# One hybrid decoder layer: two weight rings of six slots, the low part written over the raw weights, in place of three rings of four

## The reference, cut to what matters

```python
h = rms_norm(x, norm_mix)
proj | gates = h @ w_in                       # 2048 x 3608 and 2048 x 6144
y_a, y_b, y_c = swa_attention(..), stick_breaking(..), nsa_attention(..)
merged = sum_i sigmoid(g_i) * (y_i @ w_branch_i)
x = x + merged @ w_out
h = rms_norm(x, norm_ffn)
x = x + (silu(h @ w_gate) * (h @ w_up)) @ w_down   # inner width 5632
out = rms_norm(x, norm_final)
```

## Time and profile before

| what | value |
|---|---|
| median of three runs | 1362.46 us |
| profiled execution, its own time | 1363.83 us |
| its span, first to last instruction | 1362.1 us |
| mean granted clock of TensorE | 0.999 |
| TensorE busy | 1350.7 us |
| VectorE busy | 950.6 us |
| ScalarE busy | 712.1 us |
| DMA | 261.08 MB, mean 192 GB/s |

### The profile page before, as it was taken

How to read it: one execution, slowest core, us unless ns; L and a number is a source line. 1 busy time by engine, 2 the same in 40 slices (tenths; PEclk the granted TensorE clock), 3 DMA queues, 4 the chain that set the end, 5 groups by cost and what they waited for, 6 DMA issues and landing times.

```text
span 1362.1 us, 26444 instructions
## 1 busy us (share of the span) xinstructions
PE 1350.7 (99%) x11247; PEld 1315.9 (97%) x11247; DVE 950.6 (70%) x1241; ACT 712.1 (52%) x927; POOL 44.8 (3%) x70
## 2 busy tenths in 40 slices
PE   8999999999999999999999999999999999999997
PEld 7888999999999999999999999999999999999997
DVE  6554456667654756767899899985546899988554
ACT  6333356656545664455655655544344555555444
POOL 3000010000000110000000000000000000000111
PEclk9999999999999999999999999999999999999999
DMA  7776555544565667555566666656556666666653
GB/s 244 248 229 223 181 170 156 155 140 141 156 188 167 194 204 225 182 187 171 185 194 197 220 195 190 198 197 208 199 189 189 196 214 191 194 192 230 211 194 124
DMA packets 135264, 261.08 MB, mean 192 GB/s; under 512 B 8448, under 2 KB 25408, under 8 KB 134768
## 3 DMA queue, kind: packets, MB, share of 16 engines
q1 hardware_dynamic: 132912, 251.13, 57.8%
q0 software_dynamic: 1792, 7.57, 1.6%
q10 hardware_dynamic: 448, 0.76, 0.2%
HBM read 257.33 MB, written 2.10 MB: 190 GB/s over the span
## 4 chain that ended last, share of the span: by engine, by line
PE 98%; DMA 1%; DVE 0%; ACT 0%; issue 0%; ACTq 0%; DVEq 0%
PE bank L649 26%; PE bank L651 25%; PE bank L650 25%; PE bank L888 5%; PE bank L891 5%; PE bank L890 5%; PE bank L637 3%; PE bank L787 1%; PE bank L698 1%; DMA raw_ring<-in_w_in 0%; DMA sigmoid_gates<-in_norm_mix 0%; PE bank L747 0%; PE bank L1011 0%; PE bank L699 0%; PE bank L835 0%; PE bank L813 0%
## 5 line engine op out<-in xcount | busy, mean ns | idle before, releaser
L1327 DVE TENSOR_TENSOR weight_lo_ring<-raw_ring,weight_hi_ring 128x1024 fp32r<-128x1024 f32 (+2 forms) x479 | 582.3, 1221 | 317.9 <-ACT weight_hi_ring L1071 260.4
L1071 ACT ACTIVATE weight_hi_ring<-raw_ring 128x1024 fp32r<-128x1024 f32 (+2 forms) x431 | 450.6, 1050 | 459.3 <-PE bank L651 299.5
L649 PE MATMUL bank<-weight_hi_ring,hT_hi 128*128 128x256 f32 (+2 forms) x1276 | 380.9, 298 | 0.0
L651 PE MATMUL bank<-weight_hi_ring,hT_lo 128*128 128x256 f32 (+2 forms) x1276 | 375.5, 294 | 0.0
L650 PE MATMUL bank<-weight_lo_ring,hT_hi 128*128 128x256 f32 (+2 forms) x1276 | 375.5, 294 | 0.0
L649 PEld LDWEIGHTS bank<-weight_hi_ring,hT_hi 128*128 128x128 f32 x1276 | 239.8, 188 | 10.0 <-issue 3.4
L650 PEld LDWEIGHTS bank<-weight_lo_ring,hT_hi 128*128 128x128 f32 x1276 | 239.9, 188 | 6.1
L651 PEld LDWEIGHTS bank<-weight_hi_ring,hT_lo 128*128 128x128 f32 x1276 | 239.6, 188 | 6.3
L649 PE MATMUL bank<-weight_hi_ring,h2T_hi 128*128 128x256 f32 x704 | 195.5, 278 | 0.0
L650 PE MATMUL bank<-weight_lo_ring,h2T_hi 128*128 128x256 f32 x704 | 194.6, 276 | 0.0
L651 PE MATMUL bank<-weight_hi_ring,h2T_lo 128*128 128x256 f32 x704 | 194.6, 276 | 0.0
(11 more groups left out here) (253 smaller groups left out, 1933.5 us busy)
## 6 DMA issues: line engine op xcount, KB each, us to landing
raw_ring<-in_w_in SPq DMA_DIRECT2D x96, 512.0 KB, 3.5
raw_ring<-in_w_gate SPq DMA_DIRECT2D x88, 512.0 KB, 4.3
raw_ring<-in_w_up SPq DMA_DIRECT2D x88, 512.0 KB, 4.2
raw_ring<-in_w_down SPq DMA_DIRECT2D x88, 512.0 KB, 4.0
raw_ring<-in_w_in SPq DMA_DIRECT2D x55, 480.0 KB, 4.2
raw_ring<-in_w_out SPq DMA_DIRECT2D x32, 512.0 KB, 4.0
raw_ring<-in_w_br_c SPq DMA_DIRECT2D x16, 256.0 KB, 3.8
raw_ring<-in_w_br_a SPq DMA_DIRECT2D x16, 256.0 KB, 6.5
```

The lines of the kernel that those rows point to most:

```text
L649: pe.matmul(dst, x_hi, w_hi, start=opening, stop=False, skip_group_check=True)
L651: m = pe.matmul(dst, x_lo, w_hi, start=False, stop=last and k == UK - 1, skip_group_check=True)
L1071: act.activation(whi[:, s, :, 0:width(u)], raw[:, s, :, 0:width(u)], ACT.Copy)\
L1327: dve.tensor_tensor(lo, w, hi.bitcast(F32), ALU.subtract).then_inc(lo_ready, 1)
```

## The change

`RING` becomes 6. `raw` and `whi` have six slots each, and `wlo` is placed at the address of `raw`, so the low part of a unit is written over its raw weights. The space is the same, 12 slots. A slot of `raw` is now free when TensorE has used the unit: the transfer of unit u waits for `unit_used >= u - 5`, the end of unit u-6. The high part of unit u waits for the end of unit u-6 as well, and for its transfer. The number of units kept for the last part stays four (`KEPT`). The three-round loops of the input projection are gone on all four engines; units 8 to 55 go through the same written-out code as the others, with its waits (TensorE waits at each chunk for its banks to be emptied). VectorE's two waits for constants come ahead of unit 8 in place of unit 56.

```diff
--- before.py
+++ after.py
@@ -51,7 +51,8 @@
 
 
 UK = 2
-RING = 4
+RING = 6
+KEPT = 4
 UPC = KD // UK
 N_QKV = -(-N_PROJ // WQ)
 U_MIX = N_QKV * UPC
@@ -250,9 +251,10 @@
             assert top[0] <= nc.sbuf_top, name
             return t
 
+        raw_at = top[0]
         raw = place("raw_ring", [RING, UK, W])
         whi = place("weight_hi_ring", [RING, UK, W], F32R)
-        wlo = place("weight_lo_ring", [RING, UK, W], F32R)
+        wlo = at("weight_lo_ring", [RING, UK, W], raw_at, F32R)
         ident = place("identity", [P])
         gainT = place("gains_T", [4, KD])
         sumsq = place("sumsq", [TT, NC_D])
@@ -468,7 +470,7 @@
                 sp.dma_start(raw[:, slot, :, :], src).then_inc(raw_ready[slot], 16)
 
             def free(count):
-                sp.wait_ge(lo_ready, count)
+                sp.wait_ge(unit_used, count)
 
             def straight(u):
                 q, j = CHUNK_OF[u]
@@ -504,22 +506,11 @@
                 cols = slice(X_PIECES[n][0], X_PIECES[n][1])
                 sp.dma_start(X[:, :, cols], x_b[:, :, cols]).then_inc(x_ready[n], 16)
 
-            for n in range(RING):
+            for n in range(len(X_PIECES)):
                 xload(n)
-                if n > 0:
+                if 0 < n < len(X_PIECES) - 1:
                     straight(n)
-            xload(RING)
-            for u in range(RING, UPC):
-                straight(u)
-            with sp.Fori(0, (N_QKV - 2) // 2) as i:
-                for c in range(2):
-                    for j in range(UPC):
-                        u0 = UPC + c * UPC + j
-                        sp.wait_ge(lo_ready, i * (2 * UPC) + (u0 - RING + 1))
-                        sp.dma_start(raw[:, u0 % RING, :, 0:WQ],
-                                     win_b[:, UK * j:UK * j + UK, bass.ds(i * (2 * WQ) + (1 + c) * WQ, WQ)])\
-                          .then_inc(raw_ready[u0 % RING], 16)
-            for u in range(U_MIX - UPC, U_FFN):
+            for u in range(len(X_PIECES) - 1, U_FFN):
                 straight(u)
             for u in range(U_FFN, U_END):
                 what, i, j = FFN[u - U_FFN]
@@ -961,7 +952,7 @@
                         pe.wait_ge(added, done)
                     if c == 0:
                         pe.wait_ge(aT_lo, 2 * (HALVES[h][0] + j // 2 + 1))
-                    if i == LAST_DOWN and j >= n - RING:
+                    if i == LAST_DOWN and j >= n - KEPT:
                         return
                     pe.wait_ge(lo_ready, u + 1)
                     products(u % RING, (actT_hi, actT_lo), c % 2, j == 0, j == n - 1, UK * j,
@@ -973,7 +964,7 @@
 
                 def finishing(t, halves):
 
-                    for j in range(n - RING, n):
+                    for j in range(n - KEPT, n):
                         u = AT["down", LAST_DOWN, j]
                         if t == 0:
                             pe.wait_ge(lo_ready, u + 1)
@@ -1035,18 +1026,7 @@
                     for a in range(1, 4):
                         m = transpose(bank[2][:, KD * a:KD * (a + 1)], rows[0:KD, a, :], KD)
                     m.then_inc(gains_full, 1)
-            with pe.Fori(0, (N_QKV - 2) // 2) as i:
-                for c in range(2):
-                    q0 = 1 + c
-                    if c == 0:
-                        pe.wait_ge(squares, 2 * NC_D)
-
-                    for j in range(UPC):
-                        u0 = UPC * q0 + j
-                        pe.wait_ge(lo_ready, i * (2 * UPC) + (u0 + 1))
-                        products(u0 % RING, (hT_hi, hT_lo), q0 % 2, j == 0, j == UPC - 1,
-                                 UK * j, WQ).then_inc(unit_used, 1)
-            for u in range(U_MIX - UPC, U_FFN):
+            for u in range(UPC, U_FFN):
                 straight(u)
                 follow(u)
             for u in range(U_FFN, U_END):
@@ -1075,13 +1055,6 @@
                     if n >= 2:
                         act.wait_ge(unit_used, SEVENS[n - 2] + 1)
                     act.activation(ext_hi[:, n % 2, :, :], t_sum[:, :, :], ACT.Copy).then_inc(ext_hi_ready, 1)
-
-            def split_in_loop(u0, rounds, units, cols=W):
-
-                s = u0 % RING
-                act.wait_ge(raw_ready[s], rounds * 16 + landed(u0))
-                act.wait_ge(unit_used, units + (u0 - RING + 1))
-                act.activation(whi[:, s, :, 0:cols], raw[:, s, :, 0:cols], ACT.Copy).then_inc(hi_ready, 1)
 
             def hi_of_transposed(n, b, dst, gain):
 
@@ -1276,10 +1249,7 @@
                 if m == 5:
                     gains(2, slice(1, 4))
             root(1)
-            with act.Fori(0, (N_QKV - 2) // 2) as i:
-                for j in range(2 * UPC):
-                    split_in_loop(UPC + j, i * (2 * UPC // RING), i * (2 * UPC), WQ)
-            for u in range(U_MIX - UPC, U_END + LAG):
+            for u in range(UPC, U_END + LAG):
                 if u < U_END:
                     split(u)
                 follow(u - LAG)
@@ -1710,18 +1680,10 @@
                     split(m)
             norm(1, TT * NC_D)
             dve.wait_ge(rstd_ready, 1)
-            with dve.Fori(0, (N_QKV - 2) // 2) as i:
-                for c in range(2):
-                    for j in range(UPC):
-                        u0 = UPC + c * UPC + j
-                        split_unit(u0 % RING, i * (2 * UPC) + (u0 + 1), WQ)
-                        if j == LAG - 1:
-                            dve.wait_ge(unit_used, i * (2 * UPC) + UPC * (1 + c))
-                            empty_projection(c, bass.ds(i * (2 * WQ) + c * WQ, WQ))
             dve.wait_ge(consts_ready, 1)
             dve.wait_ge(sinks_ready, 16)
 
-            for u in range(U_MIX - UPC, U_END + LAG):
+            for u in range(UPC, U_END + LAG):
                 if u < U_END:
                     split(u)
                 if u == U_MIX + LAG:
```

## The result

| | before | after |
|---|---|---|
| median of 18 runs each, us | 1362.41 (1361.87 to 1364.67) | 1365.18 (1363.40 to 1368.65) |
| profiled execution, its own time / span, us | 1363.83 / 1362.1 | 1366.62 / 1364.9 |

The ratio is 1.0019, 95% interval 1.0012 to 1.0025: 2.6 us slower, the interval lying on both sides of the 0.2% that the prediction took as no change. The forecast was 1363.9 with a range of 1361.0 to 1367.5.

A forecast was written before the change was run, and what follows sets the result against it. TensorE, busy 1350.7 of 1362.1 us, was taken as the bound, with one 0.3 us wait behind its first 7 us. Terms of 1.0 + 0.4 = 1.4 us on a median of 1362.46 gave 1363.9, range 1361.0 to 1367.5.

The forecast's parts named there:

- Pace of products: All weight units: reading low parts from the buffer that transfers fill costs 0, bounds 1.2 us gained to 1.2 lost.
- low part in place: VectorE writing the low part over the raw weights takes as long as into another tile: price 0.
- Loop written out: Input projection, units 8 to 55: the jumps cost nothing, so price 0, bounds 0 to 0.3 us.
- What moves: Steady units: requests go out 3.0 us later, yet low parts are ready 7.7 us before use, against 5.8.
- Place 1: End of the input projection: later request for unit 66 delays the transposes at L736, +1.0 us, bounds -0.3 to +1.4.
- Place 2: Second load of x, at 502.94 us: unit 171's weights queue behind it and may land late, cost 0.4 us (0 to 1.1).
- Place 3: Nine gate and up rounds with VectorE busiest: slack 1.5 us, priced 0, or 4.5 us if transfers take 5.4.
- Rival A: Gate and up rounds: above about 5.0 us latency each of nine loses the excess, 1368.4 us with 5.4; chance 0.14.
- The sum: Whole kernel: 1.0 + 0.4 = 1.4 us slower, median 1363.9 us; chance of the forecast 0.60.
- own bounds: Whole kernel: the gains of the terms give 1361.0 us, their losses 1366.5 us.
- The slow stretch at 682 us: 682 to 707 us: 213 products at 0.117 us each, some 1.2 us over the usual pace, unexplained, following late low parts.

The follow-up runs named there:

- e3: Changed kernel with seven slots for raw and low part and five for the high part: 1363.47 us, ratio to the kernel before 0.9999.
- e4: Changed kernel with eight slots for raw and low part and four for the high part: 1362.88 us, ratio to the kernel before 0.9995.
- e2: Kernel before, loops written out, three rings of four, each transfer also held until the end of unit u-6: 1365.18 us, ratio 1.0015.
- e1: Kernel before with only its loops written out, three rings of four, requests as before: 1363.74 us, ratio 0.9999.
- both e6: Kernel before, loops written out, low part of unit 340 made four or five extra times: 1363.6 us (ratio 1.0000) and 1367.06 us (1.0031).
- e8: Kernel before, loops written out, low parts of six down units (326 to 356) each made five extra times: 1370.0 us, ratio 1.0045.
- e10: Changed kernel with the projection's last chunk emptied one unit earlier, behind the low part of unit 65: 1363.65 us, ratio to the kernel before 1.0004.
- e11: Changed kernel as it is, run again beside the kernel before on the same chip: 1365.14 us, ratio 1.0014.
- e6_late_5: Kernel before, loops written out, low part of unit 340 made five extra times, about 0.6 us late: 1367.06 us, ratio 1.0031.
- e5: Changed kernel with five slots in each of its two rings, ten in all: 1390.71 us, ratio to the kernel before 1.0205.

## Why the prediction was right, and where it was not

- **Pace of products, 0, and low part in place, 0:** right. 179 products in 20 us as before, at 580 and at 720 us; e3 and e4 are in place and lose nothing. In the steady state of these kernels TensorE reads the buffer that transfers fill, so they now test the Trainium skill's rule ("SBUF — State Buffer", section "SBUF: two separate sides"), and it agrees: the same 179.
- **Loop written out, 0:** right, 0.9999 (0.9990 to 1.0008). The Trainium skill ("Runtime: NRT & Kernel Launch", section "Instruction fetch mechanics") would have given a gain if the loop's first page were no longer held at the jump; the measurement shows none above 0.1%.
- **What moves:** right. The median latency at 750 to 900 us fell from 4.4 to 3.7 us, the largest from 6.7 to 4.8. In the evenly spaced stretch the largest rose, 3.9 to 4.8. The summary of the raw ring's transfers, 940 to 1020 us and then 750 to 900, against the earlier trace rows:

```profile
DMA to landing us min/median/max: 3.4/3.6/4.8
...
DMA to landing us min/median/max: 3.5/3.7/4.8
```

- **Place 1, +1.0 (bounds -0.3 to +1.4):** right, and the largest term of the sum. The request came at 165.82 (predicted 165.8), the landing after 4.62 us, the wait is 0.9 (predicted 0.8 to 1.7); unit 65 is 0.63 us longer in one profiled execution and 1.22 in another. With the late request (these two and e2) it takes 4.53 to 5.14 us, with the old one (before, e1, both e6, e8) 3.69 to 4.22. Removing the wait gives 1.5 us back (e10 against e11), of which some 0.4 was lost before as well (unit 65: 3.92 for 3.55).
- **Place 2, +0.4 (0 to 1.1):** the upper half of the bounds was too high. Unit 171 landed at 514.1 and not at 515 to 517, and its lead is 2.7 us; unit 172's grew from 1.8 to 3.1 us. The cost is 0. ScalarE's rows, against the earlier trace rows:

```profile
514.14 1.06 ACT L1051 ACTIVATE weight_hi_ring<-raw_ring 128x1024 fp32r<-128x1024 f32 x1 [7.26 <-DMA raw_ring<-in_w_in]
516.49 1.06 ACT L1051 ACTIVATE weight_hi_ring<-raw_ring 128x1024 fp32r<-128x1024 f32 x1 [1.29 <-PE bank L642]
518.72 1.06 ACT L1051 ACTIVATE weight_hi_ring<-raw_ring 128x1024 fp32r<-128x1024 f32 x1 [1.17 <-DMA raw_ring<-in_w_br_a]
```

- **Place 3, priced at 0:** this term was mis-sized. By the prediction's arithmetic the slack is 1.5 us at a latency of 3.6 and 0.3 at the 4.76 that one round had, and that round had 0.18 left. But the price was read from the median latency, while nine rounds draw nine latencies and one of them comes near the largest. And the loss begins before that slack is gone, for the slack was counted to 791.5, the end of unit 269 as it is seen, and the next product starts at 791.29, 0.2 us earlier. The loss is about 0.17 us for a unit at leads of 0.17 to 0.27, hitch and slow steps together. Such units were one in the first profiled execution of the change, two in e10 and none in e11 (whose smallest lead is 0.37): 0 to 0.3 us. In the first of these the slow pace set in behind it, 1.6 us more, but e1 has as long a stretch of it without the change. Rival A is right in kind, and at most 1.9 of its 4.5 us were seen.
- **Left out of the sum:** the 0.25 us of the last output transfer.
- **The sum:** predicted 1.4, measured 2.8 and 1.3 in the two profiled executions, 2.6 and 1.9 by the ratios. Place 1 alone was taken nearly at its full size (0.9 in the mean of the two executions), and place 2 took nothing. Place 1, the output and the hitches make 1.1 to 1.5 us by the profiles; the rest of what the medians lose, some 0.4 to 1.5 us, is not placed by them, save by the slow stretch of one execution. The measured 1365.18 lies inside the own bounds (up to 1366.5) without any part of A. In part that was luck: the bounds held 1.2 us for the pace and 1.1 for place 2 that were meant for other things, and they stood in for place 3 and the output.
- **The slow stretch at 682 us** stood in the prediction as unexplained, 1.2 us. Behind a low part with a lead of 0.2 us stands a slow stretch there too, which was a sign of what place 3 could cost.

**What stays open.** What sets the slow pace, and what ends it. A lead or a wait does not decide it alone: unit 229 has a lead of 0.22 in e6_late_5 and no slow stretch follows (223 products from 682 to 707 us), 0.22 in e11 and one does. One of e8's six waits had it. Whether late low parts make it more frequent was not shown. Nor was it shown that the timed runs spread upwards by 2 to 4 us because of it, since only profiled executions have a trace. The clock is a rival: of the 18 runs of the change the four with a mean granted clock of 0.995 to 0.997 took 1365.9 to 1367.0 us, though the longest, 1368.65, has 0.998, and e5 shows a fall of the clock soon after a wait. Nor was a version tried that cures both places with six slots each.

## What to carry to other kernels

When a buffer's release moves from an early reader to a late one, count from the new release to the use at each place where the steady rhythm is broken, and take the largest latency of the profile there, not the median: the waits and hitches of this change lie in two such places, and no steady unit waits. A ring split unevenly (eight slots for what is fetched, four for what is made on the chip) gave the memory of the change and none of its loss. And an engine that shows 99% busy can still be losing: compare the number of instructions in equal stretches.

## What the runs showed of the hardware that was not expected

- Products of 256 columns come every 0.113 us or every 0.118, with the granted clock at 1.00 in both, for one unit (e10, 286) to some 70 us (e1). The slower pace begins behind a hitch or a wait of TensorE (0.07 us lost at unit 286 of e10, 0.17 at unit 270, 0.83 at unit 338 of e8) and ends at a later break, be it a wait (e8, 994 us) or transposes (709 us; 836 us). It does not come behind every hitch, and transposes do not always end it (e1, 709 us).
- A wait of TensorE costs some 0.28 us more than its row says (six waits of 4.4 us, 6.1 us lost), since the row starts at the modelled end of the last product and the second product after it comes 0.22 us behind the first.
- An operand that is ready just when its product is due is already late: 0.17 us on the unit (low part of unit 270 ended at 791.93, product due at 791.93, started at 791.99, the next one 0.22 behind it), with no row in the list of waits.
- The last transfer of the output took 0.25 us longer in all three profiled executions with the two rings of six.
